# Spreading the modulation product over the input projections, by the tile counter, and not behind them by the clock of the planner

## What is computed

```python
def second_block(x, c, norm_g, w_ada, b_ada, w_in, ...):
    c_act = jax.nn.silu(c)
    mod = c_act @ w_ada[l] + b_ada[l]          # 1024 x 3072
    shift, scale, gate = jnp.split(mod, 3, axis=-1)
    h = rms_norm(x, norm_g[l]) * (1.0 + scale[:, None, :]) + shift[:, None, :]
    ...
    x = x + gate[:, None, :] * (y @ w_out[l])
```

```python
    h = rmsnorm(x, norm_mix_g[l])
    p = h @ w_in[l]                            # 1024 tokens x 2824 columns
    attn_out = sliding_window_attention(aq, ak, av, attn_sinks[l], slopes)
    mqk = jax.nn.silu(causal_depthwise_conv(p[..., o2:o3], conv_qk_w[l], conv_qk_b[l]))
    m_h = mlstm_chunkwise(mq, mk, mv, gif[..., :H], gif[..., H:])
    mlstm_out = (jax.nn.sigmoid(mo) * m_h).astype(x.dtype)
    x = x + jnp.concatenate([attn_out, mlstm_out], axis=-1) @ w_out[l]
```

## Time and profile before

| | |
|---|---|
| median of 3 runs | 2465.62 us (2464.94 to 2467.51) |
| the profiled execution | 2467.51 us, its span 2465.7 us |
| TensorE (PE) busy in the span | 2337.6 us, 95% |
| VectorE (DVE) | 1473.5 us, 60% |
| ScalarE (ACT) | 941.5 us, 38% |
| transfers | 238 MB, 97 GB/s |
| loads of w_ada | 12 of 1 MB, issued from 302.0 to 374.5 us, 5.1 us to landing |

### The profile page before, as it was taken

One profiled execution on the slowest core, in us unless ns is written; L12 is line 12 of the kernel. 1 busy time (PEld: TensorE's weight loads), 2 busy tenths in 40 slices (PEclk: granted clock), 3 DMA queues, 4 the chain that ended last, 5 costly groups with the idle time before them and its releaser, 6 DMA issues.

```text
span 2465.7 us, 40870 instructions
## 1 busy us (share of the span) xinstructions
PE 2337.6 (95%) x17678; PEld 1909.9 (77%) x17678; DVE 1473.5 (60%) x2442; ACT 941.5 (38%) x1524; POOL 79.0 (3%) x61
## 2 busy tenths in 40 slices
PE   7999988999999999999999999899999998889879
PEld 5777767888888888888878888687778776777757
DVE  5566856565445876777653556564455558676643
ACT  4446432444333433333332424543223233333341
POOL 0000000000000000000000000020000004000000
PEclk9999989999999999999999999899999998999989
DMA  5232243443114232223364443333223113001034
GB/s 176 86 95 69 78 156 102 147 135 113 50 54 146 60 94 86 77 77 93 119 198 140 138 133 91 115 110 119 67 61 103 42 44 124 22 24 43 2 121 153
DMA packets 329341, 238.01 MB, mean 97 GB/s; under 512 B 10949, under 2 KB 288581, under 8 KB 329033
## 3 DMA queue, kind: packets, MB, share of 16 engines
q1 hardware_dynamic: 326424, 229.82, 30.5%
q10 hardware_dynamic: 2736, 5.57, 0.6%
HBM read 202.33 MB, written 33.03 MB: 95 GB/s over the span
## 4 chain that ended last, share of the span: by engine, by line
PE 84%; DVE 11%; ACT 3%; DMA 2%; issue 1%; SPq 0%; ACTq 0%; DVEq 0%
PE PS L1522 15%; PE PS L1524 14%; PE PS L1523 14%; PE PS L1543 5%; PE PS L1544 5%; PE PS L1545 5%; PE PS L1937 5%; PE PS L1508 3%; PE PS L1562 1%; PE PS L1564 1%; PE PS L1563 1%; PE PS L1854 1%; PE PS L1808 1%; PE PS L1875 1%; PE PS L1783 1%; DVE SB L2131 1%
## 5 line engine op out<-in xcount | busy, mean ns | idle before, releaser
L1522 PE MATMUL PS<-SR 128*128 128x512 f32 (+2 forms) x1696 | 682.4, 402 | 40.7 <-DVE SR L2070 32.8
L1524 PE MATMUL PS<-SR 128*128 128x512 f32 (+2 forms) x1696 | 660.2, 389 | 0.0
L1523 PE MATMUL PS<-SR 128*128 128x512 f32 (+2 forms) x1696 | 660.1, 389 | 0.0
L2070 DVE TENSOR_TENSOR SR<-SB,SR 128x1024 fp32r<-128x1024 f32 (+1 forms) x240 | 288.3, 1203 | 295.4 <-ACT SR L2919 295.0
L1522 PEld LDWEIGHTS PS<-SR 128*128 128x128 f32 (+1 forms) x1696 | 320.7, 189 | 126.3 <-DVE SR L2070 35.1
L1524 PEld LDWEIGHTS PS<-SR 128*128 128x128 f32 (+1 forms) x1696 | 320.5, 189 | 68.6
L1523 PEld LDWEIGHTS PS<-SR 128*128 128x128 f32 (+1 forms) x1696 | 321.3, 189 | 62.0 <-issue 1.7
L2919 ACT ACTIVATE SR<-SB 128x1024 fp32r<-128x1024 f32 (+1 forms) x240 | 247.2, 1032 | 246.9 <-DMA SB<-in_w_down 115.8
L1543 PE MATMUL PS<-SR 128*128 128x512 f32 x624 | 243.4, 390 | 0.3 <-DVE SR L2196 0.3
L1545 PE MATMUL PS<-SR 128*128 128x512 f32 x624 | 242.8, 389 | 0.0
L1544 PE MATMUL PS<-SR 128*128 128x512 f32 x624 | 242.8, 389 | 0.0
(11 more groups left out here) (305 smaller groups left out, 2905.9 us busy)
## 6 DMA issues: line engine op xcount, KB each, us to landing
SB<-in_w_in SPq DMA_DIRECT2D x110, 512.0 KB, 3.8
SB<-in_w_up SPq DMA_DIRECT2D x88, 256.0 KB, 3.2
SB<-in_w_out SPq DMA_DIRECT2D x32, 512.0 KB, 3.8
SB<-in_w_down SPq DMA_DIRECT2D x32, 512.0 KB, 3.6
SB<-in_w_ada SPq DMA_DIRECT2D x12, 1024.0 KB, 5.1
hidden<-SB SPq DMA_DIRECT2D x22, 512.0 KB, 3.4
SB<-hidden SPq DMA_DIRECT2D x43, 256.0 KB, 5.5
asides<-SB SPq DMA_DIRECT2D x36, 256.0 KB, 2.6
```

The source lines that it names most:

```text
L1522: pe.matmul(out, whi[:, k - k0, :], hi[k], start=(k == 0), stop=False)
L1523: pe.matmul(out, whi[:, k - k0, :], lo[k], start=False, stop=False)
L1524: i = pe.matmul(out, wlo[:, k - k0, :], hi[k], start=False, stop=(k == j.K - 1))
L2070: v.tensor_tensor(m.f32r(a, kn * cn), m.f32(a, kn * cn), m.f32r(a + 1024, kn * cn).bitcast(F32), SUB).then_inc(*on("split.v", p))
```

## The change

The steps of ada begin no longer after the mark "g" and then every 6 us of planned time. Step i is emitted as soon as the tile counter has reached 5 + 3i: 5, 8, 11 and so on to 38. The conditions on banks stay. Everything else is the planner's doing: all steps of the first flow are laid out anew around it, and the slabs of w_ada stand among those of w_in in the ring.

```diff
     def ada(self):
 
-        yield from self.after("g")
-        begun = self.now
         for i in range(12):
-            while self.now < begun + 6 * i:
+            while self.tile < 5 + 3 * i:
                 yield self.now + 0.5
             yield from self.room((self.banks, 2))
```

## The result

The kernel after takes **2481.16 us** (median of four runs, 2478.98 to 2481.4); the kernel before, timed beside it, 2465.28 (four runs, 2464.08 to 2467.51). The ratio is 1.0061, 95% interval 1.0045 to 1.0078: slower by more than 0.2%. I had predicted 2460.3 us and a range up to 2474. The profiled execution of after took 2482.5 us, with a span of 2480.7.

What follows compares the result with a forecast made beforehand. TensorE was taken to bound the projections, a chain across engines the gate and mLSTM stages. Terms 14.8 - 2.5 + 3.0 - 12.4 - 8.2 = -5.3 us gave a median of 2460.3 us, range 2452 to 2474.

Steps and rivals of the forecast that it cites:

- (d): Gate stage, "g" to mLSTM: shrinks from 37.4 to 25 us as about two windows finish ahead; -12.4 us.
- (e): mLSTM stage, 65.4 us: loses seven ada_mm and two weight splits, partly on the chain; -8.2 us (-3.7 to -11).
- (a): TensorE ahead of "g": twelve steps of ada_mm and ada_t at 1.23 us each, all paid; +14.8 us.
- (b): Tiles 16 to 23: steps fill TensorE's 3.3 us wait for normalised input; -2.5 us (0 to -3.3).
- (c): Projections: ada slabs in the ring make splits late, ada_t waits for the row copy; +3 us (0 to +12).
- first rival: Projections: late-split waits replace the gain, 1.5 us a step, 18 us in place of 3; median 2475; chance 0.19.
- second rival: Gate stage: no window gets ahead of "g", so only 2.4 us are gained there; median 2470; chance 0.10.
- third rival: Behind "g": idler TensorE drops its clock, mLSTM average 0.95 to 0.82, some 4 us longer; median 2464; chance 0.13.

Runs made afterwards that it cites:

- filler run: Before's order, modulation steps taken out except twelve groups of 64 matmuls on a tile always on chip, against before: 2463.0 us, ratio 0.998.
- splits later: After's order with no modulation executed, but ACT and DVE split each of the first 46 slabs one slab later: 2475.12 us.
- slots and the lead kept: After's order with modulation slabs and four short matmuls each, but splits look ahead by projection slabs only: 2465.39 us.
- slots alone: After's order, twelve modulation slabs in the ring with four short matmuls each, no row copy or ada_t, against before: 2472.09 us, ratio 1.0018.

## Why the prediction was wrong, step by step

The path from before to after, in medians, each stretch from one experiment: before 2466.6; steps out of the tail 2460.8 (-5.8, or -6.9 against the before of its own set); planned order of after 2456.4 (-4.4); work put among the projections 2474.1 (+17.7); its slots 2481.2 (+7.1). In all +14.6. My sum had 14.8 - 2.5 for the work, +3 for the slots and -20.6 for everything behind "g". The same path by the marks of the profiled executions:

| kernel | "g" at | "g" to mLSTM | mLSTM to out0 |
|---|---|---|---|
| before | 319.1 | 37.4 | 67.2 |
| before's order, steps out | 320.2 | 35.4 | 62.0 |
| after's order, steps out | 317.5 | 32.8 | 62.8 |
| with the work, no slots | 335.3 | 34.0 | 61.9 |
| after | 342.5 | 33.9 | 61.8 |

Up to out0 after is 19.8 us later than my sum: 8.1 ahead of "g" (work 5.4, slots 4.2, less 1.6 that the order gained), 8.9 in (d) and 2.8 in (e).

- **(a)** was too small by 3 us. The rows gave the time from the start of an ada_mm to the start of its successor, 1.03 us, and I took it for its price. Between projection matmuls 0.2 us come with each small group, and TensorE was busy 18.0 us longer for the twelve steps, not 14.8.
- **(b)** failed. No 2.5 us were absorbed: the work alone cost 17.7 us, and TensorE's idle time was 3.0 us without it and 2.7 with it. The wait of 3.3 us was indeed gone, but in after's order it is absent with nothing executed too (its TensorE waits there are others). I had taken a wait's disappearance as proof of absorption; it isn't.
- **(c)** named the late split, but had the wrong victim and too small a size: +3 predicted, +7.1 measured on top of the work, inside my bounds of 0 to 12. I had priced the stop of TensorE at ada_t behind the row copy; in after that shows once, 1.1 us, and the waits are those of projection matmuls for their own late splits, 4.8 us. The nearest row I had taken (2.7 us for twelve ada_t) was of a stage with only two splits. I had also written that today a split finds its data landed, where ACT had waited six times, 21.5 us. A slot shortens the lead of the two splits behind it and delays three fetches, and slots without the work cost about 11 us. The first rival, the wait of (c) in place of the gain, came nearest; but at 2475 it was still 6 us short.
- **(d)** is the largest error: -12.4 predicted, -3.5 in the profile. I had turned 10 us of DVE time into "two windows" and a stage as long as the gates' chain. One window got ahead, and the planner put both that were left behind the gates' matmuls. It is so with nothing executed, too. The steps' absence gives 2.0 us (37.4 to 35.4), near the 2.4 of my second rival, in which no window gets ahead; the order gives 2.6 more, and 1.1 are lost again with the work.
- **(e)** was half right: -8.2 predicted, -5.4 in the profile (65.4 to 60.0 to the last L2580), and -5.2 to out0 with nothing but the steps taken out of before (67.2 to 62.0). Inside its bounds. The matmuls of all twelve steps, in both stages, were worth 2.2 us net of the clock, less than the 3.7 us that I gave to three with their ada_t. How the rest divides among splits, rows and slabs was not tried.
- **The clock**, my third rival, did fall as it said: PEclk 0.66 and 0.85 in the two stages, where the earlier trace rows have 0.82 and 0.95. But its price isn't shown. The filler run has more full clock and is no faster; it also has the matmuls to execute. The Trainium skill, "TensorE: Matmul & The Clock Gate", section "HAM oscillation", describes such throttling by short bursts; the granted clock in this trace agrees with it (44.4 us of low clock behind "g", before 27.3), the time does not follow from it here.
- **Not in my sum at all**: the planner's other order. The change is one line in a program that orders everything else by estimated times. Planned as in after and as in before, with the same operations executed, the kernels differ by 4.4 us; and two plans of before without modulation (planned anew, and the kept order) by 4.4 us as well. With the whole computation executed the order alone gives 6.3 us (4.2 to 9.1). In the gate stage the order gives 2.6 us (35.4 to 32.8), more than the steps' absence, and this can be had without the move. Why the order is better was not tried.

From out0 on every kernel executes the same, and yet this rest takes from 2040.2 to 2047.0 us in the profiled executions (2048.6 with splits later). What of it belongs to a kernel and what to one execution is not shown; differences of a few us between two medians carry it.

## What to carry to other kernels

An operation that brings its own weights costs a place in the ring, and here the place cost 7 us on top of 18 us of work: count what stands behind it in every in-order queue, and let the engines that prepare weights look ahead by slabs that they prepare, not by places. Price a small group among large matmuls from the last neighbour before it to the second behind it, not from its own start to the next. Split a schedule change into order, slots and work by planning one thing and executing another; a kernel with the work taken out of a fixed order tells more than one that is planned anew. And keep a plan apart from the work in it: here the planned gaps were worth having, and the work in them was not, so the best whole kernel plans the gaps and does the work later.

## Not expected of the hardware

- Twelve transfers of 128 KB in place of 1 MB in the ring changed the median by 0.9 us (2472.09 to 2471.17) and, with the work, by nothing (2482.64 to 2483.39), although the DMA share of the stage from 110.8 to 165.5 us is 0.49 with the large ones, where the like stage in the earlier trace rows has 0.35.
- The low clock behind "g" did not order the times: 41.0 us at 2460.81, 27.3 at 2463.0, 30.7 at 2460.58 (the steps behind "g" in after's order), 51.2 at 2456.41 (that order with nothing executed).
- A change between projection matmuls (128x512) and a small group on TensorE costs about 0.1 us on each side: 0.32 and 0.34 us between starts where it is 0.23 otherwise. For twelve ada_mm and ada_t that made 3 us.
- ACT stood 68 us for landings ahead of "g" in the kernel with slots and the lead kept, and 41.5 us with slots alone; TensorE's idle time was 3.7 us in the first and 11.3 in the second.
